# Relative bias rows written to the scratch array in the first layer, and tiles shifted by 32 bytes

## Chip, cores and metric

The kernel runs on one core of a Trainium2 chip. The metric is the device time of one execution in microseconds. The kernel before took 1156.61 us (median of 3 runs, 1151.21 to 1156.76).

## The reference

Two blocks run one after the other on 256 tokens of width 1024, all in float32.

The first block has two layers. Each normalizes, projects to queries, keys and values, attends over the tokens (layer 1 with a distance penalty and a window, layer 2 with a learned bias table over a 4 x 64 grid), attends with four more heads over 256 memory tokens, projects back, and runs a gated feed-forward network of width 2816. The second block is different:

```python
proj = jnp.dot(xn, w_in[l]) + b_in[l]
q, k, v, qi, ki, wi, xr, yr, gate_a, gate_b = jnp.split(proj, cuts, axis=-1)
# an indexer scores every pair (query s, key t) with 8 small heads
dots  = einsum('bqhd,bsd->bqhs', qi, ki) * 64 ** -0.5
score = einsum('bqh,bqhs->bqs', wi * 8 ** -0.5, relu(dots))     # causal, then top_k keeps 64 keys
# attention over the kept keys, with a bias by distance
bucket = t5_bucket(tb[None, :, None] - sel)                     # 32 buckets of distances
bias   = rel_bias[bucket]                                       # rel_bias is (32, 8)
p = softmax(q k / 8 + bias)
# beside it a short convolution and a gated linear recurrence on xr and yr;
# both results are projected, gated, summed, projected again, and a gated
# convolutional feed-forward network of width 2816 follows
```

What matters here is `bias`: it depends on the distance of query and key and on the head, and on nothing that the kernel computes. It can be made at any time.

## The kernel before

**Matmuls.** A float32 weight is loaded in pieces of at most 128 x 2048 into one of 4 `raw` buffers by SyncE (line 1958; a load waits until VectorE or GpSimd has read the piece four before it). ScalarE rounds it to `hi` (line 1172), VectorE (sometimes GpSimd) makes the rest `lo = raw - hi` (lines 1600, 1840), with 3 buffers for each. Each 128-row tile of the product is then three matmuls with 512 columns moving (lines 852 to 854): activations-high by hi, activations-high by lo, activations-low by hi. The activations are the stationary operand, 128 x 128 at a time. They stand in `xTh/xTl` (input of a projection), `memTh/memTl` (memory tokens), `qyh/qyl` (attention output, for `w_out`), `hTh/hTl` (feed-forward, for `w_down`), `keep` with `rTl` (recurrence and merged output in the second block) and `q2yh/q2yl` (attention output of the second block).

**Order.** A planner (`Order`) writes one list of steps before the program is built, and every engine walks the same list in order and does its share of each step. Big products are put down as parts with gaps; in each gap a small step is taken from a queue `later`, or, in the second block, from the list of names beside each column range of `IN2` (line 38). A small step that passes through PSUM takes one of 8 banks from a queue of free banks and gives it back.

**The relative bias.** `rel_bias` is turned into one row of 512 values for each head by a product with a constant one-hot table. Before the change this is the step `rel` in the first range of `IN2`:

```python
    e.wait_ge(d_rel, 32)                                                   # TensorE
    e.matmul(claim(step)[0:8, :], rel[:, :], onehot, start=True, stop=True).then_inc(x_full, 1)
    e.tensor_copy(relrow, x_bank(step)[0:8, :]).then_inc(x_dve, 1)         # VectorE
    e.dma_start(bass.AP(a["scratch"].tensor, 0, [[512, 8], [4096, 128], [1, 512]]),   # GpSimd's queue
                relrow.unsqueeze(1).to_broadcast([8, 128, 512])).then_inc(d_scr, 16)
```

The write copies each row 128 times into `scratch` in device memory (2 MB). Four later reads, steps `bias0` and `bias1`, fetch it with a skew, so that each query row gets its own shift. The table `rel` and `onehot` are loaded by GpSimd's queue in step `block2` (lines 1896, 1897). `onehot` lies in the tile `acc` and `relrow` in the tile `left`. Both are wanted again by the indexer: its heads `h0` to `h7` (`ihead`) put the rectified scores of even heads in `dist` and of odd heads in `left` (ScalarE, line 1268) and sum them in `acc` (VectorE, lines 1735, 1738). So ScalarE waits at `h0` for the write to have landed:

```python
    if h == 0:
        e.wait_ge(d_scr, 16)
```

**The placement in SBUF.** Tiles are put one after another. Up to and with `keep` every one is a multiple of 128 bytes long. `cols` has 1,248 bytes, `small` 704. Behind them come `junk`, `ones`, 4 `stats`, 9 `rms` (1,024, 512, 4 x 64 and 9 x 64 bytes), and then the tiles that share room from stage to stage: `early`, `mkT`, `mv`, `memT`, `qy`, `kT`, `v`; `big`; `hT`; and in the second block `rTl`, `acc`, `left`, `sgb`, `rel` (32 bytes), `stage2`, `wi` (64 bytes), `q2y`, `k2T`, `v2`.

Of the kernel before, what the change touches and what calls it, by code (L numbers as in the profile page):

```python
# [33 lines left out]
def tiles_of(n):  # L34
    return [(c, min(512, n - c)) for c in range(0, n, 512)]


IN2 = [("qi", 768, 512, ["gates", "rel", ""]),
# [94 lines left out]
class Order:  # L133
# [299 lines left out]
    def mix(self, l):  # L433
# [10 lines left out]
        self.later.extend(steps)  # L444
        if l == 0:
            self.linear("mem", 1, 0, 512, 2, "mem", 1)
        made = []
# [20 lines left out]
    def run(self):  # L468
# [4 lines left out]
        self.later.append(("memsq",))  # L473
        self.later.append(("rows",))
        for j in range(2):
            self.pieces(0, j)
# [75 lines left out]
def build(nc, a, out):  # L552
    ctx = ExitStack()
    with ctx:
# [54 lines left out]
        cols = sb("cols", [128, 128 + 96 + 88])  # L609
        small = sb("small", [128, 176])  # L610
        junk = sb("junk", [128, 512], mybir.dt.bfloat16)
# [53 lines left out]
        with ExitStack() as sc:  # L665
            rTh, rTl = keep, sb("rTl", [128, 8, 256], R, sc)
            acc = sb("acc", [128, 2, 256], F, sc)[:, :, :]
            left = sb("left", [128, 2, 256], F, sc)[:, :, :]
            sgb = sb("sgb", [128, 2, D], F, sc)
            rel = sb("rel", [32, 8], F, sc)  # L670
            stage2 = [sb(f"stage{i}", [128, 2, 512], F, sc) for i in range(2)]
            wi = sb("wi", [128, 2, 8], F, sc)
            qy[2] = [sb(f"q2y{n}", [128, 4, 256], R, sc) for n in "hl"]
            kT[2] = [sb(f"k2T{n}", [128, 2, 256], R, sc) for n in "hl"]
            v[2] = [sb(f"v2{n}", [128, 2, 128], R, sc) for n in "hl"]
            p_slots[2] = [[sb(f"p2{n}{i}", [128, 2, 256], R, sc)[:, :, :] for n in "hl"] for i in range(2)]
        with ExitStack() as sc:
            hT[2] = [sb(f"hT{n}2", [128, 22, 256], R, sc) for n in "hl"]
            last_tmp = sb("lasttmp", [128, 2, 512], F, sc)
# [7 lines left out]
        conv_slot = [big[:, 2560 + 512 * i:3072 + 512 * i].rearrange("p (k t) -> p k t", k=2) for i in range(CONVS)]  # L687
        onehot = acc[0:32, :, :].rearrange("p t k -> p (t k)")
        relrow = left[0:8, :, :].rearrange("p t k -> p (t k)")
        wrg = sgb[:, :, :].rearrange("p g (n d) -> p g n d", n=8)  # L690
# [130 lines left out]
        def tensor_program(e):  # L821
            seen = set()

            def claim(name):
                await_bank(e, name)
                return x_bank(name)
# [86 lines left out]
            for step in order.steps:  # L913
# [63 lines left out]
                elif kind == "rel":  # L977
                    e.wait_ge(d_rel, 32)
                    e.matmul(claim(step)[0:8, :], rel[:, :], onehot, start=True, stop=True).then_inc(x_full, 1)
                elif kind in ("qi", "q"):  # L980
# [50 lines left out]
        def scalar_program(e):  # L1031
# [132 lines left out]
            for step in order.steps:  # L1164
# [96 lines left out]
                elif kind == "ihead":  # L1261
                    h = name[0]
                    e.wait_ge(x_full, filled(step))
                    if h == 0:
                        e.wait_ge(d_scr, 16)
                    if h >= 2:
# [532 lines left out]
        def gpsimd_program(e):  # L1799
# [33 lines left out]
            for step in order.steps:  # L1833
# [31 lines left out]
                elif kind == "att":  # L1865
                    attention(*name)
                elif kind == "rpb":
                    e.dma_start(a["scratch_rpb"], bass.AP(a["rpb_b"].tensor, 0, [[0, 64], [1, PITCH]])).then_inc(d_rep, 16)
                    e.wait_ge(d_rep, 16)
# [24 lines left out]
                elif kind == "block2":  # L1894
                    e.wait_ge(part_done, last_of["lastdown", 1] + 1)
                    e.dma_start(rel[:, :], a["rel_bias_2"]).then_inc(d_rel, 16)
                    e.dma_start(onehot, a["onehot"]).then_inc(d_rel, 16)
                    e.dma_start(wrg[:, 0, :, :], a["w_rg_2"][0].rearrange("n c d -> c n d")).then_inc(d_wg, 16)
# [166 lines left out]
```

## Time and profile before

| | |
|---|---|
| runs (median, range) | 1156.61 us, 1151.21 to 1156.76 |
| the profiled execution: its time, its span | 1151.83 us, 1150.0 us |
| mean granted TensorE clock | 0.968 |
| TensorE busy | 1069.2 us, 93% |
| VectorE busy | 727.2 us, 63% |
| ScalarE busy | 585.0 us, 51% |
| GpSimd busy | 248.1 us, 22% |
| DMA | 209.29 MB, mean 182 GB/s |

The span is the time from the first to the last instruction. PE is TensorE's matmul side and PEld its weight loads, DVE is VectorE, ACT ScalarE, POOL GpSimd, SP SyncE. The granted clock is given as a share of 2.4 GHz. The recorded end of a matmul is modelled, so where matmuls follow each other closely the distance of their starts tells their pace. Stages by time: memory and input projections of layer 1 up to 82 us, its attention to 134 us, its feed-forward to 342 us; layer 2 to 652 us; the second block from there, with the feed-forward's last product from 1065 to 1140 us.

### The profile page before, as it was taken

Reading aid. Unit: us, or ns where it says so; the run is one execution under the profiler, and the core shown is the slowest. Engines: PE = TensorE matmul, PEld = TensorE weight load, DVE = VectorE, ACT = ScalarE, POOL = GpSimd, SP = SyncE. Lnnn points to the kernel's source line nnn. Section 1 sums busy time; section 2 is a strip of 40 time slices with the busy share of each in tenths; the row PEclk is TensorE's granted clock in tenths of the full one; section 3 lists DMA queues with packets and bytes.
Section 4 is the critical chain, followed back from the end, with each engine's and each line's share of the span. In section 5 each row is a group of like instructions: output and inputs, shape, how many; then the busy total and the mean of one; then the engine's idle time right before and its main releaser. Section 6 shows DMA issues by size and latency. Waiting matters only on the chain.

```text
span 1150.0 us, 13564 instructions
## 1 busy us (share of the span) xinstructions
PE 1069.2 (93%) x5224; PEld 878.5 (76%) x5224; DVE 727.2 (63%) x943; ACT 585.0 (51%) x834; POOL 248.1 (22%) x212
## 2 busy tenths in 40 slices
PE   6998999999999999999999995598999979999996
PEld 5877877888787887888787874487777778778885
DVE  5667774545455675697976751559866764566853
ACT  6547653443445475543443350368655456565631
POOL 0012144500000031432231130012550022333101
PEclk8999999999999999999999998699999989999999
DMA  9640389555555413789988856445453535445440
GB/s 328 215 146 1 110 208 285 180 184 165 198 186 180 151 41 103 246 300 351 325 299 308 284 125 108 139 149 159 162 192 111 183 129 183 146 153 187 155 165 37
DMA packets 97825, 209.29 MB, mean 182 GB/s; under 512 B 5649, under 2 KB 13281, under 8 KB 94625
## 3 DMA queue, kind: packets, MB, share of 16 engines
q1 hardware_dynamic: 93313, 194.46, 50.0%
q0 software_dynamic: 4288, 13.89, 5.6%
q8 instruction: 42, 0.69, 0.2%
q14 instruction: 22, 0.18, 0.1%
q10 hardware_dynamic: 160, 0.07, 0.0%
HBM read 205.25 MB, written 4.57 MB: 182 GB/s over the span
## 4 chain that ended last, share of the span: by engine, by line
PE 64%; DVE 12%; DMA 9%; ACT 6%; issue 4%; POOL 3%; SPq 1%; DVEq 0%; ACTq 0%; POOLq 0%
PE bank L852 19%; PE bank L854 18%; PE bank L853 18%; DMA scratch<-left 4%; DVE lo L1600 4%; PE bank L830 4%; ACT hi L1172 3%; DMA raw<-in_w_gate_up 3%; DVE big L1612 2%; DMA raw<-in_w_ada 1%; PE bank L832 1%; PE bank L865 1%; POOL lo L1840 1%; PE bank L966 1%; DMA small<-in_sink_a 1%
## 5 line engine op out<-in xcount | busy, mean ns | idle before, releaser
L1600 DVE TENSOR_TENSOR lo<-raw,hi 128x2048 fp32r<-128x2048 f32 (+1 forms) x146 | 335.8, 2303 | 197.2 <-ACT hi L1172 196.5
L1172 ACT ACTIVATE hi<-raw 128x2048 fp32r<-128x2048 f32 (+1 forms) x164 | 303.7, 1853 | 210.7 <-PE bank L854 131.8
L852 PE MATMUL bank<-hi,xTh 128*128 128x512 f32 (+2 forms) x896 | 347.8, 388 | 1.1 <-DVE lo L1600 0.9
L854 PE MATMUL bank<-hi,xTl 128*128 128x512 f32 (+2 forms) x896 | 338.3, 378 | 0.0
L853 PE MATMUL bank<-lo,xTh 128*128 128x512 f32 (+2 forms) x896 | 338.0, 377 | 0.0
L852 PEld LDWEIGHTS bank<-hi,xTh 128*128 128x128 f32 x896 | 171.1, 191 | 34.0 <-issue 2.0
L854 PEld LDWEIGHTS bank<-hi,xTl 128*128 128x128 f32 x896 | 170.5, 190 | 31.8
L853 PEld LDWEIGHTS bank<-lo,xTh 128*128 128x128 f32 x896 | 171.0, 191 | 28.6 <-issue 0.2
L1840 POOL TENSOR_TENSOR lo<-raw,hi 128x2048 fp32r<-128x2048 f32 x18 | 87.2, 4843 | 252.2 <-ACT hi L1172 252.2
L852 PE MATMUL bank<-hi,hTh 128*128 128x512 f32 x264 | 105.0, 398 | 2.7 <-DVE lo L1600 2.3
L853 PE MATMUL bank<-lo,hTh 128*128 128x512 f32 x264 | 104.3, 395 | 0.0
L854 PE MATMUL bank<-hi,hTl 128*128 128x512 f32 x264 | 104.2, 395 | 0.0
L1612 DVE SCALAR_TENSOR_TENSOR big<-raw,small,big 128x2048 f32<-128x2048 f32 x24 | 85.8, 3583 | 12.6 <-DMA raw<-in_w_ada 8.7
L852 PEld LDWEIGHTS bank<-hi,hTh 128*128 128x128 f32 x264 | 49.5, 188 | 15.3 <-DVE lo L1600 2.7
L854 PEld LDWEIGHTS bank<-hi,hTl 128*128 128x128 f32 x264 | 49.5, 187 | 12.1
L853 PEld LDWEIGHTS bank<-lo,hTh 128*128 128x128 f32 x264 | 49.5, 188 | 11.6
L1589 DVE SCALAR_TENSOR_TENSOR big<-bank,cols,big 128x255 f32<-128x255 f32 (+2 forms) x100 | 41.1, 474 | 20.3 <-ACT big L1338 16.7
L1802 POOL TENSOR_TENSOR rms<-rms,small 128x2 f32<-128x2 f32 x9 | 6.4, 709 | 209.4 <-DVE rms L1367 185.2
L830 PE MATMUL bank<-const,nrm 128*128 128x128 f32 x201 | 35.7, 290 | 13.6 <-DVE nrm L1698 6.8
L830 PEld LDWEIGHTS bank<-const,nrm 128*128 128x128 f32 x201 | 27.0, 149 | 22.1 <-DVE nrm L1698 7.3
L830 PE MATMUL bank<-const,stage 128*128 128x128 f32 x52 | 9.7, 297 | 34.2 <-DVE stage L1549 30.4
L1037 ACT ACTIVATE junk<-xres 128x512 bf16<-128x512 f32 x32 | 20.2, 632 | 40.3 <-DVE xres L1532 29.3
(351 smaller groups left out, 1471.9 us busy)
## 6 DMA issues: line engine op xcount, KB each, us to landing
raw<-in_w_gate_up SPq DMA_DIRECT2D x44, 1024.0 KB, 5.6
raw<-in_w_down SPq DMA_DIRECT2D x30, 1024.0 KB, 5.8
raw<-in_w_ada SPq DMA_DIRECT2D x24, 1024.0 KB, 6.7
raw<-in_w_up SPq DMA_DIRECT2D x22, 1024.0 KB, 5.2
raw<-in_w_in SPq DMA_DIRECT2D x21, 1024.0 KB, 5.0
raw<-in_w_out SPq DMA_DIRECT2D x12, 1024.0 KB, 5.0
raw<-in_w_in_b SPq DMA_DIRECT2D x10, 1024.0 KB, 5.1
raw<-in_w_in_a SPq DMA_DIRECT2D x6, 1024.0 KB, 9.7
```

Of the source, the lines that this page charges most:

```text
L830: e.transpose(bank[:, i * 128:(i + 1) * 128], x, ident)
L832: e.transpose(bank[:, n * 128:(n + 1) * 128], blocks[n], ident).then_inc(x_full, 1)
L852: e.matmul(o, sh, h[:, k, :], start=p.first and k == 0, stop=False)
L853: e.matmul(o, sh, lo[:, k, :], start=False, stop=False)
L854: done = e.matmul(o, sl, h[:, k, :], start=False, stop=p.last and k == p.nk - 1)
L865: e.matmul(o, qh, k[0], start=True, stop=False)
L1037: e.activation(junk[:, :], x, ACT.Square, accum_out=rms[i][:, 2 * j + t:2 * j + t + 1]).then_inc(squared, 1)
L1172: e.activation(hi_s[m % SPLITS][:, 0:n], raw[p.at % RAWS][:, 0:n], ACT.Copy).then_inc(hi_made, 1)
L1589: e.scalar_tensor_tensor(out=o[:, j, n:], in0=bank[:, j * 256:j * 256 + 256 - n], scalar=weights[j][n - 1], in1=o[:, j, n:], op0=ALU.mult, ...
L1600: e.tensor_tensor(lo_s[s][:, 0:n], raw[p.at % RAWS][:, 0:n], hi_s[s][:, 0:n].bitcast(F), ALU.subtract).then_inc(lo_dve, 1)
L1612: e.scalar_tensor_tensor(out=piece, in0=raw[i % RAWS][:, :], scalar=small[:, k:k + 1], in1=piece, op0=ALU.mult, op1=ALU.add).then_inc(ada_ ...
L1840: e.tensor_tensor(lo_s[s][:, 0:n], raw[p.at % RAWS][:, 0:n], hi_s[s][:, 0:n].bitcast(F), ALU.subtract).then_inc(lo_pool, 1)
```

## The change

The loads of `rel` and `onehot` become a step `relload` of the first layer, on GpSimd's queue, as soon as the rows at the start of `early` have been used. The step `rel` stands between the query projection of layer 1 and the memory projection for layer 2. The rows stand in `early` and `small` instead of `acc`, `left` and a tile of their own. ScalarE's wait at `h0` is gone; GpSimd waits for the write ahead of step `rpb` instead, since that step loads into room over `early`. `small` grows by 32 bytes, `rel` as a tile of 32 bytes goes, `wi` moves behind `p_slots[2]`.

```diff
-IN2 = [("qi", 768, 512, ["gates", "rel", ""]),
+IN2 = [("qi", 768, 512, ["gates", "", ""]),
@@ mix
         self.later.extend(steps)
         if l == 0:
+            self.put("rel")
             self.linear("mem", 1, 0, 512, 2, "mem", 1)
@@ run
         self.later.append(("rows",))
+        self.later.append(("relload",))
@@ build
-        small = sb("small", [128, 176])
+        small = sb("small", [128, 184])
...
-            rel = sb("rel", [32, 8], F, sc)
             stage2 = [sb(f"stage{i}", [128, 2, 512], F, sc) for i in range(2)]
-            wi = sb("wi", [128, 2, 8], F, sc)
             qy[2] = [sb(f"q2y{n}", [128, 4, 256], R, sc) for n in "hl"]
...
             p_slots[2] = [[sb(f"p2{n}{i}", [128, 2, 256], R, sc)[:, :, :] for n in "hl"] for i in range(2)]
+            wi = sb("wi", [128, 2, 8], F, sc)
...
-        onehot = acc[0:32, :, :].rearrange("p t k -> p (t k)")
-        relrow = left[0:8, :, :].rearrange("p t k -> p (t k)")
+        onehot = early[0:32, 2048:2560]
+        relrow = early[0:8, 2560:3072]
+        rel = small[0:32, 152:160]
@@ tensor_program
-                    e.matmul(claim(step)[0:8, :], rel[:, :], onehot, start=True, stop=True).then_inc(x_full, 1)
+                    e.matmul(claim(step)[0:8, :], rel, onehot, start=True, stop=True).then_inc(x_full, 1)
@@ scalar_program
-                    if h == 0:
-                        e.wait_ge(d_scr, 16)
@@ gpsimd_program
+                elif kind == "relload":
+                    e.wait_ge(x_full, filled(("rows",)))
+                    e.dma_start(rel, a["rel_bias_2"]).then_inc(d_rel, 16)
+                    e.dma_start(onehot, a["onehot"]).then_inc(d_rel, 16)
                 elif kind == "rpb":
+                    e.wait_ge(d_scr, 16)
...
                 elif kind == "block2":
                     e.wait_ge(part_done, last_of["lastdown", 1] + 1)
-                    e.dma_start(rel[:, :], a["rel_bias_2"]).then_inc(d_rel, 16)
-                    e.dma_start(onehot, a["onehot"]).then_inc(d_rel, 16)
```

## Rows read from the trace of the kernel before

**Rows 1.** The page: busy time, share of the span and instructions of each engine.

```profile
PE 1069.2 (93%) x5224; PEld 878.5 (76%) x5224; DVE 727.2 (63%) x943; ACT 585.0 (51%) x834; POOL 248.1 (22%) x212
```

**Rows 2.** Chain of waits around 679 us: start us, us, what.

```profile
679.15 45.78 DMA scratch<-left
```

**Rows 3.** Who waited for whom, 640 to 800 us: total us, times, longest us.

```profile
ACT const L1268 <- DMA scratch<-left: 32.3, 1, 32.3
```

**Rows 4.** Timelines of ACT, then PE: start us, us, instruction [idle before <-releaser].

```profile
692.37 0.38 ACT L1159 ACTIVATE k2Th<-bank 128x256 fp32r<-128x256 f32 x1 [1.06 <-PE bank L832]
725.02 0.60 ACT L1268 ACTIVATE const<-bank 128x512 f32<-128x512 f32 x1 [32.27 <-DMA scratch<-left]
...
705.14 0.39 PE L854 MATMUL bank<-hi,xTl 128*128 128x512 f32 x1
731.78 0.90 PE L830 MATMUL bank<-const,stage 128*128 128x128 f32 x3 [26.25 <-DVE stage L1549]
```

**Rows 5.** Stretches: length, busy us (instructions) by engine, granted clock, DMA share, GB/s.

```profile
705.50:731.70 26.20, 0.03 (x1) 0.00 (x0) 4.87 (x8) 4.68 (x4) 0.00 (x0) 0.54 0.50 102
731.70:738.30 6.60, 6.51 (x19) 5.19 (x20) 5.44 (x10) 1.62 (x3) 0.54 (x1) 0.50 0.95 333
735.00:760.00 25.00, 25.00 (x120) 19.96 (x119) 13.96 (x25) 14.35 (x20) 0.00 (x0) 0.93 0.39 126
```

**Rows 6.** Weight loads (L1958) issued 676 to 735 us, then 60 to 125 us.

```profile
DMA to landing us min/median/max: 5.0/37.0/38.8
...
DMA to landing us min/median/max: 5.1/5.1/5.2
```

**Rows 7.** Timelines of PE, DVE and POOL: the step `rel` where it stood.

```profile
676.50 1.02 PE L979 MATMUL bank<-acc,rel 32*8 32x512 f32 x2
...
677.56 0.68 DVE L1717 COPY left<-bank 8x512 f32<-8x512 f32 x1 [6.01 <-PE bank L979]
...
679.15 1.12 POOL L1911 DMA_DIRECT2D scratch<-left  x1 [12.25 <-DVE left L1717]
```

**Rows 8.** Layer 1: a stretch, and timelines of PE, ACT and POOL.

```profile
90.00:100.00 10.00, 8.55 (x62) 7.07 (x62) 7.38 (x28) 7.85 (x26) 2.76 (x6) 1.00 0.00 0
...
69.22 0.39 PE L852 MATMUL bank<-hi,memTh 128*128 128x512 f32 x1
...
133.31 1.92 ACT L1172 ACTIVATE hi<-raw 128x2048 fp32r<-128x2048 f32 x1
...
151.26 0.63 POOL L1868 DMA_DIRECT2D scratch_rpb<-in_rpb_b  x1
```

**Rows 9.** Timeline of PE: every ninth or sixth start, in four products.

```profile
211.00 0.39 PE L852 MATMUL bank<-hi,xTh 128*128 128x512 f32 x1
...
213.04 0.39 PE L852 MATMUL bank<-hi,xTh 128*128 128x512 f32 x1
...
285.18 0.40 PE L852 MATMUL bank<-hi,hTh 128*128 128x512 f32 x1
...
287.28 0.39 PE L852 MATMUL bank<-hi,hTh 128*128 128x512 f32 x1
...
882.14 0.40 PE L852 MATMUL bank<-hi,keep 128*128 128x512 f32 x1
...
884.23 0.39 PE L852 MATMUL bank<-hi,keep 128*128 128x512 f32 x1
...
904.92 0.40 PE L852 MATMUL bank<-hi,q2yh 128*128 128x512 f32 x1
...
906.32 0.40 PE L852 MATMUL bank<-hi,q2yh 128*128 128x512 f32 x1
```

**Rows 10.** Stretches of three feed-forward down products, columns as in Rows 5.

```profile
300.00:335.00 35.00, 35.00 (x155) 27.96 (x154) 17.74 (x13) 13.55 (x14) 0.00 (x0) 1.00 0.51 166
600.00:630.00 30.00, 29.56 (x127) 23.46 (x126) 19.95 (x10) 10.18 (x13) 6.83 (x2) 1.00 0.80 298
1100.00:1140.00 40.00, 40.00 (x174) 32.09 (x172) 16.80 (x12) 11.87 (x10) 2.59 (x2) 1.00 0.19 67
```

## Prediction

> **What bounds the kernel now.** The page says first that TensorE is busy for 1069.2 of the 1150.0 us of the span [rows 1]. So time can come from two places only: the 80.8 us in which TensorE does nothing, and the pace of its matmuls. This change touches both.
>
> The chain of waits shows the largest single piece of the idle time. It is no engine but one DMA, the write of the bias rows into the scratch array: 45.78 us from 679.15 us on, so it lands at 724.93 us [rows 2]. The list of who waited for whom says who stood behind it: ScalarE at line 1268, the first indexer head, for 32.3 us, once [rows 3]. The timelines show how that reaches TensorE. ScalarE ended its last job at 692.75 us and took up the first head at 725.02 us. Everything behind that head in its order stood still: the rounding of the next weights to `hi`, and with it VectorE's `lo` and VectorE's sum of the heads. TensorE had matmuls ready up to 705.53 us and then waited 26.25 us, until 731.78 us, for VectorE to empty the projection `xr`, which is behind those sums in VectorE's order [rows 4]. The clock then adds to it: in the gap and up to 738.3 us the granted clock is 0.50 of 2.4 GHz, so that the first 6.6 us of work after the gap go at 1.2 GHz [rows 5].
>
> The weight loads say that the write did more harm than the wait. Those issued from 676 to 735 us took 37.0 us in the median and up to 38.8 us to land, where those of the first layer's attention took 5.1 us [rows 6]. The write and these loads share the DMA engines. So if only the wait were taken out, a load issued near 681 us could still land near 719 us. The write has to go from there, and it does.
>
> **The change part by part.**
>
> *The wait at the first head goes.* ScalarE can do that head when its scores are there, about 696 us. I followed the three engines from there with the durations of the trace: head 0 on ScalarE 0.6 us, the next `hi` 1.9 us, `lo` 2.3 us, so ready near 701 us, well ahead of the part that wants it. Head 1 has its scores near 700 us, VectorE empties `xr` by 704 us. TensorE reaches the transposes that wait for it at 705.4 us. It would not stop. What is late next is nothing that I can name: in 735 to 760 us, with two to three heads per part as here, TensorE is busy for all of 25.00 us while VectorE needs 13.96 and ScalarE 14.35 [rows 5]. So the gap of 26.25 us goes, and half of the 6.6 us at 0.50, which is 3.3 us. Together 29.55 us. I take off 0.5 us for small waits at the seams: 29.0 us.
>
> *The step `rel` moves.* At its old place it costs TensorE 1.02 us, VectorE 0.68 us and GpSimd's queue 1.12 us for the issue [rows 7]. TensorE works without a break there, so 1.0 us goes. At the new place, between two products, at 69.22 us, TensorE works without a break as well [rows 8], so 1.0 us comes. Nothing is left over. VectorE's copy falls into its wait for the next `hi`. The three issues on GpSimd's queue (two loads at about 20 us, the write at about 71 us) stand behind the row step and ahead of the first root and of the scaling of the attention weights, where GpSimd has nothing to do. The loads of 1 KB and 64 KB cost what the 1.1 us of issue costs, on an idle engine. The product could also find its PSUM bank not yet emptied, since it takes the one that has been free longest: from 0 to 1.3 us, and I take 0. The bank queue is one place on for a few steps and then as before. In the second block 1.1 us of issue goes from in front of two loads that GpSimd does early enough either way; I take 0.
>
> *The write now runs beside the first layer's attention.* It starts near 71.5 us; with the same 45.8 us it lands near 117 us. There the DMA engines have nothing to do: share 0.00 in 90 to 100 us. Two weight loads are issued while it runs, near 74 and 81 us. If each took 38.8 us, they would land near 113 and 120 us. Their `hi` are made at 133.31 us and 141 us, so 20 us of cover are left. The new wait on GpSimd is in front of `rpb`, which it begins at 151.26 us, 34 us after the landing [rows 8]. Behind that wait stand only the table's own loads. Cost: nothing, up to a write of about 65 us.
>
> *The tiles move by 32 bytes.* Counted from `xTh`, which is followed only by multiples of 128 bytes up to `cols`: `cols` and `small` make 1,952 bytes, the small tiles behind them 2,368 bytes, together 4,320, which is 96 past a multiple of 128 (32 past one of 64). All shared tiles begin there. `rel` and `wi` add 96, so that `q2yh` is at 64. After the change every one of them is at a multiple of 128. Is there a price for that in the trace? The pace of products with 512 columns, by the distance of starts at the full clock [rows 9]:
> - `xTh/xTl` (at 0): nine matmuls in 2.04 us, 226.7 ns each.
> - `hTh/hTl` (at 96): nine in 2.10 us, 233.3 ns.
> - `q2yh/q2yl` (at 64): six in 1.40 us, 233.3 ns.
> - `keep` twice and `rTl` (at 0, 0, 96): nine in 2.09 us, 232.2 ns.
>
> The moving operand, the banks and the loops are alike, so the place of the stationary tile is the best reading. The last line speaks a little against it: two of three are well placed there and yet it is slow; it could be that one bad load in three breaks the pace of all. 6.7 ns a matmul is the gain, if placing is the cause. How many: 3 x 264 = 792 for `hT` (22 tiles of rows, 2 halves, 2 column ranges, 3 products, three times), 96 for `memT`, 192 for `qy`, 192 for `keep/rTl`, 48 for `q2y`: 1,320, at most 8.8 us. Not all of it is on the path. In the first and last of the down products TensorE is busy all the time (35.00 of 35, 40.00 of 40), so 528 x 6.7 ns = 3.5 us count in full. In layer 2's the DMA share is 0.80 and TensorE has gaps [rows 10]; a faster TensorE waits for weights there, and I take half of 1.8 us. Of the other 528 (3.5 us) I take 2.4 us, since the first 48 wait for loads and a part of the `w_out` product follows the attention. Sum 6.8 us; bounds 0 and 8.8 us. Some 500 matmuls with 256 columns have such tiles too, most of them in attentions, where TensorE has gaps (8.55 of 10.00 us busy) [rows 8]: between 0 and, at the same 6.7 ns, 3.3 us; I take 0. Other engines read and write the moved tiles as well, and no row tells the places apart for them: 0.
>
> The Trainium skill bears on this in "SBUF — State Buffer", under "Door 1: The DMA port swizzle", in the note on cachelines: a line has 16 bytes, and crossing into a new one is what costs. Places 96, 64 and 0 all begin such a line, so by that rule the shift is worth 0 and the total 1122.8 us. The trace shows three paces by place, and I go by the trace.
>
> Total: 29.0 + 6.8 = 35.8 us. The profiled execution took 1151.83 us, so 1116.0 us. The runs of before lie at 1151.21 and at about 1156.7 us, the profiled one near the lower, the median (1156.61) at the upper; I put the prediction 1 us above, at 1117 us.
>
> **The rivals.**
>
> 1. *Placing is worth nothing.* For it: the `keep` line. Then 29.0 us are left: 1151.83 - 29.0 = 1122.8 us. The skill's rule above says the same.
>
> 2. *The gap is partly given back.* After the release ScalarE and VectorE had 6.76 us of stored-up work before TensorE went on (725.02 to 731.78 us) [rows 4]. If this doesn't fit beside TensorE's matmuls, up to 6.8 us come back: 1122.8 us. Against it: the two engines are idle for 32 us in that time.
>
> 3. *The late weight loads are not the write's doing.* If loads in this stage take 38.8 us for another reason, the one issued near 681 us lands near 719.7 us instead of being met at 725.0 us, and only 5.3 us of the gap go: 1151.83 - 5.3 - 6.8 = 1139.7 us. For it: I infer the cause only from the two stretches. Against it: the only large thing on the DMA engines that differs is the write.
>
> 4. *Slower: the write holds up the first layer.* GpSimd, which issues the write, is in use in the attention, and the write might take much longer there. From 65 us on every microsecond comes on top, as the `hi` at 133.31 us waits for its load and ScalarE holds all behind it. The kernel is slower than before from a write of 65 + 35.8 = 101 us on; at 110 us it would be 1151.83 - 35.8 + 45 = 1161 us. Against it: GpSimd has 2.76 of 10 us to do there [rows 8].
>
> **How the numbers follow.** The forecast case has 0.58, rival 1 0.22, rival 2 0.12, rival 3 0.05, rival 4 0.03. Range: low end with all of 8.8 and 29.55 us and the 1 us of `rel` at the old place, from the fastest run: 1151.21 - 39.4 = 1111.9, and 2 us for what I can't see: 1110 us. High end with no gain by placing, from the upper runs: 1156.76 - 29.0 = 1127.8, and 1 us for the bank: 1129 us. That takes in rivals 1 and 2. About 0.5% (5.8 us) is what a measurement of this kernel can tell from no change. Faster by more than that are all but rival 4 and a little of rival 3: 0.96; within it 0.01; slower 0.03.
>
> **What would show it right or wrong.** Right: no line 1268 behind a DMA, and TensorE busy in all of the stretch where the projection `xr` ends; no granted clock of 0.50 there; loads in that stage land in 5 to 6 us; the write near 71 us, landing before 120 us; the `hT` matmuls 226.7 ns apart. Wrong: a new gap of TensorE in front of the transposes of `xr`, loads that still take over 30 us there, `hT` at 233.3 ns, or a `hi` near 133 us that waits for a load.

## The result and the profile after

The changed kernel takes 1117.86 us (median of 4 runs, 1116.45 to 1118.92), the kernel before 1155.16 us in the same comparison. The ratio is 0.9684, with a 95% interval from 0.9657 to 0.9711, or 36.5 us less (here and below, "us less" is what the ratio takes off the median of the kernel before; the medians themselves differ by 37.3 us). The forecast was 1117 us. The span of the profiled execution fell from 1150.0 to 1115.5 us.

Three rows of the page of the kernel after: the span, the busy times, and the shares of the chain that ended last.

```profile
span 1115.5 us, 13564 instructions
...
PE 1061.2 (95%) x5224; PEld 877.7 (79%) x5224; DVE 728.7 (65%) x943; ACT 584.6 (52%) x834; POOL 246.7 (22%) x212
...
PE 69%; DVE 11%; issue 6%; ACT 6%; DMA 4%; POOL 3%; SPq 1%; ACTq 0%; DVEq 0%; POOLq 0%
```

Against [rows 1] TensorE is busy for 8.0 us less (1069.2 to 1061.2), and idle for 26.5 us less (80.8 to 54.3). The idle part is the gap. The busy part is mostly the pace: with the tiles moved alone TensorE is busy for 1064.7 us, with the step moved alone for 1067.5 us, where less work runs at the half clock. (The lines of the changed kernel stand two to three lower: 852 to 854 are now 854 to 856, the weight loads of 1958 are 1961.)

ScalarE at the old place of the wait, in the timeline of the kernel after:

```profile
690.42 0.39 ACT L1161 ACTIVATE k2Th<-bank 128x256 fp32r<-128x256 f32 x1 [1.06 <-PE bank L834]
...
694.07 0.60 ACT L1268 ACTIVATE const<-bank 128x512 f32<-128x512 f32 x1 [3.26 <-PE bank L869]
```

Head 0 waits 3.26 us for its own scores, where it stood 32.27 us behind a DMA [rows 4]. Next the stretch in which TensorE stood still (length, busy us by engine, granted clock, DMA share, GB/s):

```profile
705.00:735.00 30.00, 30.00 (x148) 24.20 (x149) 20.02 (x33) 18.01 (x24) 0.54 (x1) 1.00 0.40 130
```

TensorE is busy for all of it at the full clock of 2.4 GHz; before it had a gap of 26.25 us and a granted clock of 0.50 [rows 5]. Now the weight loads of the kernel after, issued from 676 to 735 us and then from 60 to 125 us:

```profile
DMA to landing us min/median/max: 4.9/5.0/5.3
...
DMA to landing us min/median/max: 5.1/21.0/37.1
```

And the write, in the list of DMA issues (KB each, median us to landing):

```profile
scratch<-early POOLq DMA_DIRECT2D x1, 2048.0 KB, 44.1
```

The two stretches of [rows 6] have changed places: the slow loads went with the write. It is issued at 71.4 us, lands 44.1 us later, at 115.5 us, and the weight loads under it (issued at 74.0 and 81.7 us) take 37 us. The roundings that need them start at 135.70 and 143.34 us, so nobody waits.

### The profile page after: what moved, and what is told of

Same layout as the page of the kernel before. It is cut to its first block, busy times and chain, and to the rows that moved or that the text cites. A ratio compares the mean times of both kernels' runs of the same rounds, so it can differ in the third digit from the quotient of the medians.

```text
span 1115.5 us, 13564 instructions
## 1 busy us (share of the span) xinstructions
PE 1061.2 (95%) x5224; PEld 877.7 (79%) x5224; DVE 728.7 (65%) x943; ACT 584.6 (52%) x834; POOL 246.7 (22%) x212
## 4 chain that ended last, share of the span: by engine, by line
PE 69%; DVE 11%; issue 6%; ACT 6%; DMA 4%; POOL 3%; SPq 1%; ACTq 0%; DVEq 0%; POOLq 0%
PE bank L854 20%; PE bank L856 19%; PE bank L855 19%; PE bank L832 4%; ACT hi L1174 3%; DVE lo L1600 3%; DMA raw<-in_w_gate_up 2%; DVE big L1612 2%; POOL lo L1840 2%; DMA raw<-in_w_ada 1%; PE bank L867 1%; PE bank L834 1%; PE bank L968 1%; POOL big L1948 1%; PE bank L868 1%
## 5 line engine op out<-in xcount | busy, mean ns | idle before, releaser
L1600 DVE TENSOR_TENSOR lo<-raw,hi 128x2048 fp32r<-128x2048 f32 (+1 forms) x146 | 336.8, 2309 | 202.0 <-ACT hi L1174 201.4
L1174 ACT ACTIVATE hi<-raw 128x2048 fp32r<-128x2048 f32 (+1 forms) x164 | 303.7, 1853 | 202.7 <-PE bank L856 128.9
L832 PE MATMUL bank<-const,nrm 128*128 128x128 f32 x201 | 36.1, 292 | 13.7 <-DVE nrm L1698 7.0
L1884 POOL TENSOR_TENSOR big<-big,const 128x256 f32<-128x256 f32 x24 | 28.4, 1225 | 16.9 <-DMA big<-scratch_rpb 16.9
```

The source lines that it names most:

```text
L832: e.transpose(bank[:, i * 128:(i + 1) * 128], x, ident)
L1174: e.activation(hi_s[m % SPLITS][:, 0:n], raw[p.at % RAWS][:, 0:n], ACT.Copy).then_inc(hi_made, 1)
L1600: e.tensor_tensor(lo_s[s][:, 0:n], raw[p.at % RAWS][:, 0:n], hi_s[s][:, 0:n].bitcast(F), ALU.subtract).then_inc(lo_dve, 1)
L1884: e.tensor_tensor(bias[:, h, n, :], bias[:, h, n, :], window, ALU.add).then_inc(window_added, 1)
```

## Experiments

Twelve kernels ran. In each comparison the kernel before ran beside them; its medians were 1153.4 to 1155.6 us. "Span" is that of the profiled execution.

### The parts of the change, one by one

**Only the tiles moved (e1_place).**

```diff
-        small = sb("small", [128, 176])
+        small = sb("small", [128, 184])
...
-            rel = sb("rel", [32, 8], F, sc)
...
+        rel = small[0:32, 152:160]
...
```

(`wi` goes behind `p_slots[2]`; the step `rel` stays where it was.)

> Only the placement: small grows by 32 bytes, rel goes into small, wi moves to the end; the step rel, its write and the wait of the first indexer head stay where they were. If the place of the stationary tile sets the pace, the 512-column matmuls on hT, qy, keep/rTl and q2y come every 226.7 ns instead of 233.3, and the kernel gains 3.5 us (first and last down product) to 6.8 us, about 5 us. If the place is worth nothing: 0 us, and hT stays at 233.3 ns. The gap of TensorE near 700 us stays 26 us in either case.

1145.98 us, ratio 0.9934 (0.9914 to 0.9954), 7.6 us less; span 1146.4 us. Placing alone is worth something, and leaves the gap: TensorE still stands for 24.06 us, until 730.63 us. The span fell by only 3.6 us (1150.0 to 1146.4), so the size of this part is known no better than its interval, 5.3 to 9.9 us, says.

**Only the step moved (e2_move).** The change with 32 bytes of `small` taken back and given to a spare tile, so that all shared tiles begin as before.

```diff
-        small = sb("small", [128, 184])
+        small = sb("small", [128, 176])
...
+            gap = sb("gap", [32, 8], F, sc)
...
```

> Only the move of the bias rows; every tile stays where it was (a gap of 32 bytes in the place of rel). The forecast's theory: the gap of 26.25 us and half of the 6.6 us at half the clock go, the kernel gains 29 us, and hT stays at 233.3 ns. The rival that the gap is partly given back: 22 us. In the first layer the first weights after the attention's start are made up to 1 us later if only TensorE's 1.0 us of the step counts, 2.5 us later, as with the whole change, if the step or the write costs more there.

1126.29 us, ratio 0.9761 (0.9735 to 0.9787), 27.6 us less; span 1122.6 us. The two parts add: 7.6 + 27.6 = 35.2 us beside 36.5 us for both, well within the intervals.

**Only the wait taken out (e4_nowait).** The write stays at its old place, from a buffer that the heads don't use.

```diff
-        relrow = left[0:8, :, :].rearrange("p t k -> p (t k)")
+        relrow = big[0:8, 4096:4608]
...
-                    if h == 0:
-                        e.wait_ge(d_scr, 16)
...
```

> The kernel before, with the write of 2 MB where it was, but its source row in a part of big that nobody wants before the recurrence's gates, so that the first indexer head doesn't wait for the write (ScalarE waits for it at the first gate instead). It tells the wait from the harm to the loads. If only the wait counted, the gap goes and the gain is 29 us. If the loads beside the write land after 37 to 39 us, as before, the piece loaded near 681 us is there near 719 us, TensorE has a gap of about 14 us in front of it, and the gain is 12 to 17 us. If the wait counted for nothing: 0 to 6 us.

1148.90 us, ratio 0.9957 (0.9934 to 0.9979), only 5.0 us less; span 1146.1 us. Its timelines of ScalarE, VectorE (the `xr` bias sum) and TensorE behind it:

```profile
698.34 0.60 ACT L1266 ACTIVATE const<-bank 128x512 f32<-128x512 f32 x1 [3.28 <-PE bank L867]
...
719.84 1.91 ACT L1172 ACTIVATE hi<-raw 128x2048 fp32r<-128x2048 f32 x1 [17.04 <-DMA raw<-in_w_in]
...
726.72 1.29 DVE L1549 TENSOR_TENSOR stage<-bank,gbc 128x512 f32<-128x512 f32 x2 [22.86 <-issue]
...
728.06 0.90 PE L830 MATMUL bank<-const,stage 128*128 128x128 f32 x3 [20.23 <-DVE stage L1549]
```

The landing times of its weight loads issued from 676 to 735 us, then of the bias rows `gbc` issued from 660 to 735 us:

```profile
DMA to landing us min/median/max: 7.8/36.9/38.7
...
DMA to landing us min/median/max: 5.3/6.8/41.7
```

Head 0 runs at 698.34 us, without any wait, and TensorE still stands for 20.23 us. Two transfers hold it. A weight load lands late for the rounding at 719.84 us. And the bias row for `xr`, which GpSimd issues at 684.93 us behind the write, takes 41.7 us: 684.93 + 41.7 = 726.6 us, and VectorE's sum starts at 726.72 us. The profile calls that wait "issue"; the landing time names it. My expectation of 12 to 17 us less fell, since it reckoned with the weight load alone, which lands at 719.8 us.

**Only the write cut to an eighth (e8_eighth).** Wait, step and tiles as before.

```diff
+                elif kind == "fill":          # in the first layer's attention, rows 16 to 127
+                    e.dma_start(bass.AP(a["scratch"].tensor, 16 * 4096, ...), bass.AP(a["norm_final"].tensor, 0, ...)) ...
...
-                    e.dma_start(bass.AP(a["scratch"].tensor, 0, [[512, 8], [4096, 128], [1, 512]]),
+                    e.dma_start(bass.AP(a["scratch"].tensor, 0, [[512, 8], [4096, 16], [1, 512]]),
...
```

> The kernel before, with nothing moved: the step `rel`, the wait of the first head and the tiles stay where they were. Only the write at the old place is cut to the first 16 of its 128 rows (256 KB instead of 2 MB); the other rows of the scratch array are filled in the first layer's attention with the values of the final norm's weights, so the bias of those rows is left out. Theory A, 'the harm is the transfer of 2 MB beside the loads, and the wait is only as long as the transfer': the write lands in 6 to 10 us, before the first head has its scores, the loads of weights near it land in 5 to 8 us and those of the bias row in as little, no gap of 26 us is left, and the span is that of the kernel with the move alone (1122.6 us), 1121 to 1125 us. Rival, 'the wait itself costs what the prediction gave it': the wait is still in the program, but met; the same time, so this can't tell. Rival, 'even a small write from 8 partitions blocks the loads' : loads stay above 20 us and half of the gap remains, 1135 us or more.

1126.59 us, ratio 0.9772 (0.9741 to 0.9802), 26.3 us less; span 1123.3 us, that of the step moved alone (1122.6). The old stretch, with TensorE busy throughout:

```profile
705.00:735.00 30.00, 30.00 (x152) 24.12 (x151) 19.59 (x30) 18.66 (x25) 0.54 (x1) 1.00 0.42 139
```

Its DMAs issued from 676 to 735 us (KB each, median us to landing):

```profile
raw<-in_w_in SPq DMA_DIRECT2D x7, 1024.0 KB, 5.2
gbc<-in_b_in POOLq DMA_DIRECT2D x3, 256.0 KB, 6.5
scratch<-left POOLq DMA_DIRECT2D x1, 256.0 KB, 7.8
```

The longest of the weight loads took 9.8 us. The wait is still in the program and costs nothing. Beside the run before this one, that settles the cause: the gap was the 2 MB under way, and the wait was one of three ways in which it reached TensorE.

**The write doubled (e7_twice).**

```diff
+                    for to in ("scratch", "scratch2"):
-                    e.dma_start(bass.AP(a["scratch"].tensor, ...
+                        e.dma_start(bass.AP(a[to].tensor, ...
...
```

> The whole change with the 2 MB write issued twice, the second time into an array that nobody reads; all that waits for the write waits for both. It tests the 20 us of cover that the prediction claimed in layer 1, and its rival 4. Theory A, 'a load under the write takes some 37 us whatever the write's length, and counts only where its rounding has less cover': the two writes last to about 160 us; the `hi` of the loads issued near 74 and 82 us still starts at 135 to 144 us, but the loads issued near 119 and 132 us land near 156 and 169 us instead of being met at 152 and 157 us; so TensorE waits about 12 us near 155 to 170 us, and the span is 1125 to 1132 us. Rival 4 as the prediction put it, 'the loads land with the write': a write of 90 us is 25 us past the cover, span 1140 us. Rival 'layer 1 swallows it': the DMA-bound stretch behind makes up for nothing, as DMA engines are the limit there; if it did, the span would stay at 1116 to 1118 us.

1131.05 us, ratio 0.9815 (0.9779 to 0.9850); span 1130.3 us, 14.8 us more than the kernel after. Landing times of its weight loads issued from 60 to 125 us:

```profile
DMA to landing us min/median/max: 5.1/55.0/76.1
```

TensorE in the last part of the first layer's attention, then ScalarE with the two roundings that stood at 135.70 and 143.34 us:

```profile
136.91 0.79 PE L854 MATMUL bank<-hi,qyh 128*128 128x512 f32 x1 [7.17 <-issue]
...
142.06 0.60 ACT L1050 ACTIVATE ph<-bank 128x512 fp32r<-128x512 f32 x1 [10.39 <-PE bank L912]
...
147.34 1.92 ACT L1174 ACTIVATE hi<-raw 128x2048 fp32r<-128x2048 f32 x1
...
156.77 1.92 ACT L1174 ACTIVATE hi<-raw 128x2048 fp32r<-128x2048 f32 x1 [1.67 <-DMA raw<-in_w_gate_up]
```

The two writes take 82.3 and 87.5 us and land at 152.5 and 159.0 us. The two loads under them land at 143.6 us (issued at 72.9, 70.7 us) and at 156.8 us (issued at 80.6, 76.1 us). My expectation that a load under a write takes 37 us whatever the write's length fell; that the span came out inside its 1125 to 1132 us was luck.

The rounding at 147.34 us doesn't wait for its load, which had landed 3.8 us before. It is late because TensorE stood still for 7.17 us in the middle of a product whose operands it had just been using, and then worked until 142.7 us at a granted clock of 0.50. With a start that was already 1.5 us later (the `hi` of 127.79 us starts at 129.28 us), 7.2 us and half of the 5.8 us at 0.50, that makes the 11.6 us. The profile names no releaser for the stop. Its DMA queue `instruction` points at one: from 108.3 to 134.1 us it carries nothing, where the kernel after has four packets in that time, and TensorE goes on at 136.91 us, 1.35 us after a packet of 16 KB (134.56 to 135.56 us). So the late arrival of TensorE's own instructions, behind the two writes, is the likely cause; no run tests it.

The rounding at 156.77 us does wait for its load, and is 13.4 us late. That is most of the 14.8 us at the end, and would be there without the stop. The prediction's rival 4 was right in its direction: with a longer write the loads land later than they are needed, and the end moves. It was not right in size. It let the load land with the write and gives 87.5 - 65 = 22.5 us, but both loads landed before the second write, one of them before the first. So the cover is real, but no more than one write of this size fits in it.

### What the place of a tile costs

The pace given here is the median over all runs of ten matmuls in a row with 512 columns at the full clock, first start to tenth, divided by 9. The prediction counted places in multiples of 128 bytes. Five shifts tested that. (By this measure `xT` has 226.7 ns in the kernel after and 234.2 ns in e6; the 227.5 and 234.0 ns in the expectation of e9 are not by this measure.)

**Stationary tiles at 64 (e3_place64)** and **at 32 (e5_place32)** past a multiple of 128:

```diff
-        small = sb("small", [128, 184])
+        small = sb("small", [128, 168])
...
```

(This is e3; in e5 the length is 192.)

> The whole change, but small is 64 bytes shorter (the 16 columns for the maxima go to free columns of it), so that all shared tiles begin at 64 past a multiple of 128 bytes instead of at 0. If multiples of 64 bytes are enough, hT is at 226.7 ns a matmul and the time is that of the change, 1118 us. If it takes multiples of 128, as q2y at 64 in the kernel before says, hT is at 233.3 ns and the time is 4 to 6 us more, about 1123 us.

> The whole change, with 32 bytes more in `small`, so that every stationary tile behind it begins 32 bytes past a multiple of 128. Theory A, 'only a start at a multiple of 128 bytes gives the full pace, and any other place of these costs the same': the products of `hTh/hTl` go at 233 ns a matmul as with tiles at 96, and the span is that of the changed kernel plus 7 to 9 us, 1123 to 1125 us. Theory B, 'the price depends on the place': tiles at 64 had cost 4.5 us of span and about 229 ns a matmul, tiles at 96 some 6.7 ns each; then 32 gives a third figure, and if it falls with the distance from the end of the line of 128 bytes, it is at or under 229 ns and the span is 1117 to 1120 us. Rival, 'placing by 32 is as good as 0': 226.7 ns and 1115.5 us. The gap of TensorE at the old place of the write stays away in all three.

e3: 1122.44 us, ratio 0.9733 (0.9702 to 0.9764), span 1120.0 us, `hT` 228.9 ns. e5: 1128.17 us, ratio 0.9765 (0.9714 to 0.9817), span 1128.4 us, `hT` 233.3 ns. The 228.9 ns of e3 are neither of the two figures expected. The two runs differ, as theory B of e5 said, but not in its order: 32 is worse than 64. And `q2y`, at 64 in both, goes at 228.9 ns in e3 and at 233.6 ns in the kernel before. One place, two paces: the place of the stationary tile can't be the whole of it. (Of e5's span a part is a granted clock of 0.50 from 692.8 to 699.6 us, which the kernel after does not have there.)

**Moving operands at 32 (e6_moving)** and **at 64 (e9_moving64)**, stationary tiles at multiples of 128:

```diff
+        gap0 = sb("gap0", [128, 8])
         hi_s = ...
         lo_s = ...
+        gap1 = sb("gap1", [128, 24])
...
-        small = sb("small", [128, 184])
+        small = sb("small", [128, 152])
...
```

(This is e6; in e9 both spare tiles have 16 columns.)

> The whole change with the stationary tiles left at multiples of 128 bytes, but with the MOVING operands of the big products (`hi` and `lo`, the weights) pushed to 32 bytes past a multiple of 128 by two spare tiles. Theory A, 'it is the load of the stationary tile that the place slows': nothing happens, `hTh/hTl` stay at 226.7 ns, span 1115.5 us give or take 1.5. Theory B, 'TensorE reads any operand slower from such a place': all 512-column matmuls on `hi` and `lo` take longer, 233 ns or more in the `hT` products, and the span is at least 7 us longer, 1123 us or more. If ScalarE, VectorE and GpSimd were slowed by the place of what they write, the roundings to `hi` and `lo` would show a mean over 1.9 and 2.3 us.

> As the run with the moving operands at 32, but `hi` and `lo` at 64 past a multiple of 128 bytes; the stationary tiles stay at multiples of 128. At 32 the `xT` and `hT` products had gone at 234.0 and 233.3 ns a matmul instead of 227.5 and 226.7, and the span had grown by 12.1 us. Theory A, 'place counts for the moving operand as for the stationary one, and 64 costs less than 32 or 96' (stationary tiles at 64: 229 ns): 229 to 231 ns and a span of 1119 to 1123 us. Theory B, 'any place that is no multiple of 128 costs the same for the moving operand': 234 ns and 1126 to 1129 us. Theory C, 'it was the other tiles that this shift moved, or the chip that day': 227 ns and 1115 to 1118 us.

e6: 1129.65 us, ratio 0.9797 (0.9770 to 0.9824), span 1127.6 us; `xT` 234.2 ns, `hT` 233.3 ns. My first theory, that the load of the stationary tile is slowed, fell. The roundings are not slower for the place they write to: `hi` takes 1857 ns in the mean (1853 in the kernel after), `lo` 2296 (2309). e9: 1129.56 us, ratio 0.9783 (0.9764 to 0.9802), span 1126.7 us; `xT` 233.3 ns, but `hT` 228.9 ns. Both tiles begin at multiples of 128 there, so neither theory A nor B covers it.

**Everything at 32 (e10_all32).**

```diff
+        gap0 = sb("gap0", [128, 8])
         hi_s = [sb(f"hi{i}", [128, 2048], R) for i in range(SPLITS)]
```

> The whole change with one spare tile of 32 bytes ahead of `hi`, so that everything behind it, `hi`, `lo`, `xres`, `nrm`, `xT`, the identity and all stationary tiles, begins 32 bytes past a multiple of 128: both operands of each product are off by the same amount. Theory A, 'the absolute place counts, and one operand off is enough': 233 to 235 ns for `xT` and `hT`, nothing on top of the one-sided case, and a span of 1126 to 1130 us as with `hi` and `lo` alone at 32. Theory B, 'each operand off costs its own 6.7 ns': 240 ns, span 1137 to 1142 us. Theory C, 'it is the distance of the two operands from each other that counts': 227 ns, span 1115 to 1118 us.

1120.14 us, ratio 0.9710 (0.9686 to 0.9734), span 1116.0 us; `xT` and `hT` 226.7 ns. Theory C: what counts is the distance of the two operands from each other. That led to the last two.

**Stationary tiles at multiples of 128, 128 bytes lower (e11_dist128).**

```diff
-        small = sb("small", [128, 184])
+        small = sb("small", [128, 152])
...
```

> The whole change, with `small` cut so that the stationary tiles behind it begin 128 bytes lower; they still begin at multiples of 128. What the runs so far have in common is the distance from the start of `hi` to the start of the stationary tile, taken modulo 256: 0 gives 226.7 ns a matmul (also with everything at 32), 192 gives 228.9, 64 and 32 and 224 give 233.3, 96 gives 234.2. In the changed kernel all distances are 0; a distance of 128 was in no run. Theory A, 'the distance modulo 128 decides, with noise in between': `hT` at 226.7 ns and a span as the changed kernel, 1115 to 1117 us. Theory B, 'the distance modulo 256 decides, and 0 is the only full pace': `hT` at 229 to 234 ns and a span of 1119 to 1125 us; then the change was lucky beyond its rule of multiples of 64. The `xT` products, whose distance is 0 here too, stay at 226.7 ns in both.

**`xT` ahead of `hi` (e12_xt192).**

```diff
+        xTh = ...
+        xTl = ...
+        gap0 = sb("gap0", [128, 16])
         hi_s = ...
...
-        small = sb("small", [128, 184])
+        small = sb("small", [128, 168])
...
```

> The whole change with `xTh` and `xTl` put ahead of `hi` and 64 bytes behind them, and `small` cut by 64 bytes: `hi` now begins 64 past a multiple of 128 and all stationary tiles but `keep` at multiples of 128, as in the run with the moving operands at 64. But the distance from `hi` is 192 modulo 256 for `xT` as for `hT`, where in that run it was 64 for `xT` (233.3 ns) and 192 for `hT` (228.9 ns). Theory A, 'the distance modulo 256 decides': both go at 228.9 ns, span 1119 to 1124 us. Theory B, 'the places modulo 128 decide, and xT is slower than hT for another reason (its size, its stage)': `xT` stays at 233.3 ns, `hT` at 228.9 ns, span 1125 to 1128 us. Theory C, 'it depends on which tile comes first': another figure for `xT`, 226.7 ns or above 234 ns.

e11: 1122.37 us, ratio 0.9728 (0.9692 to 0.9765), span 1120.9 us, `hT` 232.2 ns: a multiple of 128 and yet slow. e12: 1120.32 us, ratio 0.9701 (0.9663 to 0.9738), span 1117.8 us, `xT` and `hT` both 228.9 ns. In both, theory "distance modulo 256" held for the paces; the span of e12 lies under the 1119 to 1124 us expected. The timelines of TensorE, each pair nine starts apart. Kernel after, `hT` (2.04 us):

```profile
284.95 0.39 PE L854 MATMUL bank<-hi,hTh 128*128 128x512 f32 x1
...
286.99 0.39 PE L854 MATMUL bank<-hi,hTh 128*128 128x512 f32 x1
```

Everything at 32, `hT` (2.04 us):

```profile
301.81 0.39 PE L855 MATMUL bank<-hi,hTh 128*128 128x512 f32 x1
...
303.85 0.39 PE L855 MATMUL bank<-hi,hTh 128*128 128x512 f32 x1
```

Distance 128, first `xT`, whose distance is still 0 (2.04 us), then `hT` (2.09 us):

```profile
210.64 0.39 PE L854 MATMUL bank<-hi,xTh 128*128 128x512 f32 x1
...
212.68 0.39 PE L854 MATMUL bank<-hi,xTh 128*128 128x512 f32 x1
...
284.76 0.39 PE L854 MATMUL bank<-hi,hTh 128*128 128x512 f32 x1
...
286.85 0.39 PE L854 MATMUL bank<-hi,hTh 128*128 128x512 f32 x1
```

Moving operands at 64, `xT` (2.10 us), then `hT` (2.06 us):

```profile
211.07 0.40 PE L856 MATMUL bank<-hi,xTh 128*128 128x512 f32 x1
...
213.17 0.39 PE L856 MATMUL bank<-hi,xTh 128*128 128x512 f32 x1
...
301.68 0.39 PE L856 MATMUL bank<-hi,hTh 128*128 128x512 f32 x1
...
303.74 0.39 PE L856 MATMUL bank<-hi,hTh 128*128 128x512 f32 x1
```

`xT` ahead of `hi`, `xT` (2.06 us):

```profile
210.88 0.39 PE L855 MATMUL bank<-hi,xTh 128*128 128x512 f32 x1
...
212.94 0.39 PE L855 MATMUL bank<-hi,xTh 128*128 128x512 f32 x1
```

All together, by the distance in bytes from the start of `hi` to the start of the stationary tile, modulo 256. The starts are those of the compiled programs; in the kernel before `hi` is at 49,280, `xTh` at 114,816, `hTh` at 178,016, `q2yh` at 206,784.

| distance | products | ns a matmul |
|---|---|---|
| 0 | `xT` in before, after, e1, e2, e3, e5, e11; `hT` in after, e1; both in e10 | 226.7 |
| 192 | `hT` and `q2y` in e3, e9; `xT`, `hT` and `q2y` in e12 | 228.9 |
| 128 | `hT`, `q2y` in e11 | 232.2, 232.1 |
| 32 | `hT`, `q2y` in e5 | 233.3, 233.2 |
| 64 | `xT` in e9; `q2y` in before, e2 | 233.3, 233.6 |
| 224 | `hT` in before, e2, e6 | 233.3 |
| 96 | `xT` in e6 | 234.2 |

Every distance in the table has one pace, within 0.3 ns, whichever tile and kernel it is in. In the kernel after, `xTh` is 256 x 256 bytes from `hi` and `hTh` 503 x 256; one is an even multiple and one an odd, at the same pace, so the period is 256 and not 512. Distance 160 was in no run. (e4 and e8 have the tiles and the paces of the kernel before, e7 those of the kernel after.) The tiles `lo`, `hTl` and `xTl` lie multiples of 256 from their partners, so one distance holds for all three products.

Where that is not so, the table does not give the pace. `keep` and `rTl`, the high and low parts of one operand, have the same distance in the kernel after, e1, e7 and e10 (0 for both, 226.7 ns), and two different ones in most others. In the kernel before they are at 0 and 224 and go at 231.2 ns, where two products at 226.7 and one at 233.3 would give 228.9. In e12 they are at 0 and 192 and go at 231.6 ns, slower than either distance in the table (2.09 us for nine):

```profile
858.91 0.39 PE L855 MATMUL bank<-hi,keep 128*128 128x512 f32 x1
...
861.00 0.39 PE L855 MATMUL bank<-hi,keep 128*128 128x512 f32 x1
```

So the distance of the two stationary tiles from each other seems to count as well. How it does was not tested, and what in the chip makes the distance count stays open.

## Why the prediction was right, and where it was not

**The gap (forecast 29.0 us): right in size.** In the trace of the step moved alone, the starts of the same roundings come 3.2 us later than before at 670 us and 26.25 us earlier at 700 us. That is 29.5 us at this place, with 1.0 us for the product that is no longer there; forecast were 29.0 + 1.0. No new wait came behind it, so rival 2 (a part given back) fell.

**The cause of the gap: right in the main, with one cause missing.** The prediction said that a load of the weights would hold TensorE if the wait alone went. It did (e4). It did not see the bias row on GpSimd's own queue, which lands at 726.6 us in e4; in the kernel before it was as late (issued at 684.24 us, 41.8 us to land, so at 726.0 us), only a little behind the wait's end at 724.93 us [rows 2]. Rival 3 (the late loads not the write's doing) fell with the loads of 5 us.

**The step `rel` (forecast 0): about right.** In the first layer the interval between two roundings around it grew from 6.7 us to 7.75 us and more in all kernels that have it there, so it costs the 1.0 us that was reckoned, and the old place gives the same back.

**The write in the first layer (forecast 0): right for the write.** Landing at 115.5 us (forecast 117), nobody waits. Yet the first layer's attention ended later: the `hi` of 133.31 us [rows 8] starts at 135.70 us in the kernel after and at 136.49 us with the step alone. 1 us of it is `rel`. The rest comes in the next interval and goes with how long the granted clock stands at 0.50 (1.2 GHz of 2.4) in this attention. The stretch of 85 to 100 us, in the kernel after, with the wait alone taken out (e4) and with everything at 32 (e10):

```profile
85.00:100.00 15.00, 12.93 (x73) 10.90 (x73) 10.45 (x36) 9.25 (x30) 4.45 (x10) 0.77 0.55 87
```

```profile
85.00:100.00 15.00, 14.01 (x71) 12.01 (x69) 9.57 (x33) 8.76 (x29) 3.73 (x8) 0.66 0.00 1
```

```profile
85.00:100.00 15.00, 12.59 (x88) 9.90 (x87) 11.13 (x41) 11.16 (x38) 4.66 (x10) 1.00 0.51 70
```

The third number from the end is the mean granted clock, the next the DMA share. A mean of 0.77 is 2 x 0.23 x 15 = 6.9 us at half clock; in the kernel before it is 0.89 (3.3 us), with the step alone 0.66 (10.2 us). The write is not its cause: e4 has none there (share 0.00) and a clock of 0.66; e10 has it (0.51) and the full clock. The same shows in the interval of roundings from 76.39 to 111.94 us of the kernel before, in all fourteen traces: 35.4 to 35.6 us with up to 3.4 us at 0.50 (before, e3, e6, e10, e12), 37.0 to 37.1 with 6.8 us (after, e1, e11), 38.3 to 38.5 with 10.2 us (e2, e4, e8), 39.3 to 39.6 with 13.7 us (e5, e7, e9). Kernels with the write there and without it stand in the same groups. What sets the clock stays open. It is a scatter of some 4 us in this interval that the sum had no term for.

**Placing (forecast 6.8 us, bounds 0 to 8.8): right in size, wrong in reason.** Measured were 7.6 us (5.3 to 9.9) with placing alone (3.6 us in the spans of the profiled executions), and 7.1 us of span between the step alone and the whole change. Rival 1 fell. But the step "the place of the stationary tile is the best reading" failed. What the shift changed is the distance between moving and stationary operand: 32 bytes up made 128,736 into 128,768 = 503 x 256 for `hT`, and 64 bytes down made 157,504 into 157,440 = 615 x 256 for `q2y`. With the same multiples of 128, 128 bytes lower, e11 gave back 5.4 us of span. And with no tile at a multiple of 128, e10 lost nothing (1116.0 beside 1115.5 us of span). The forecast came out by luck: in this kernel both readings name the same tiles, and the shift happened to bring all of them to distance 0. In [rows 9] `xTh`, `hTh` and `q2yh` don't tell the two readings apart, and the prediction did not name the second. It did see that the `keep` line speaks against its reading; this line fits the distance alone no better (see the text under the table).

The cacheline rule that the prediction quoted from the Trainium skill ("SBUF — State Buffer", under "Door 1: The DMA port swizzle") would have every place at a multiple of 16 bytes alike. All of the places here are, and the paces run from 226.7 to 234.2 ns. So the rule, taken for the starts of TensorE's operands as the prediction took it, does not give what these runs show.

**The sum.** 29.0 + 6.8 = 35.8 us forecast; 34.5 us in the spans of the profiled executions, 36.5 us by the ratio. Both terms were near. In the profiled pair the attention of the first layer took back 2.4 us, 1.0 of it the step `rel` and 1.4 the clock.

## What to carry to other kernels

When one large transfer is late, look beyond the engine that waits for it: list every load issued while it is under way, on its own queue too, and ask of each whether it would hold the end if the wait were gone. Here the wait alone was worth 5 us and the transfer with it 27 us; making it eight times smaller in place did as much as moving it.

Before reading a cause out of two or three addresses, write down the distance between the operands as well as their places, and find one row that tells the two apart. In this kernel a free choice of 32 bytes in an unrelated small tile is worth 7 us, and a tile put between the operands, if its length is no multiple of 256 bytes, can lose it again.

## What the runs showed of the hardware that was not expected

- The pace of fp32 matmuls with 128 x 128 stationary and 512 columns moving depends on the distance of the two operands in SBUF modulo 256 bytes: 226.7 ns at 0, 228.9 at 192, 232.2 at 128, 233.2 to 234.2 at 32, 64, 96 and 224, as long as the high and the low stationary tile have the same distance. With 0 for one and 192 for the other it is 231.6 ns. The same absolute place gave different paces, and different places with the same distance gave the same pace.
- A pace lower by 3% in nearly all big products (e6: `xT` 234.2 ns, `hT` 233.3 ns) cost 12.1 us of 1115.5, or 1.1%. From [rows 10] one can see where the rest may hide: in stretches with a DMA share of 0.80 TensorE waits for weights anyway.
- A write of 2 MB from 8 partitions into DRAM took 44.1 to 47.3 us, and 82.3 to 87.5 us when two were issued together; loads of 1 MB under them took 36 to 40 and up to 76.1 us instead of 5. In the stretch of 85 to 100 us the DMA share under a single write was 0.51 to 0.55, and under two 0.97. The fill of 1.75 MB from DRAM to DRAM in e8 took 23.3 us, and the two loads beside it 18.1 and 15.1 us.
- Under the two writes TensorE stood for 7.17 us in the middle of a product, without a releaser in the profile, and went on 1.35 us after a packet of 16 KB on the DMA queue `instruction`.
- At the same work the attention of the first layer ran with 0 to 13.7 us at a granted clock of 0.50, from one kernel to the next.
